# The router of a mixture-of-experts block rewritten: experts chosen by token blocks, one-pass count and slot products, overflow tables computed behind the first expert

## Chip, cores and metric

One core of one Trainium2 chip runs the whole kernel. The metric is device time in microseconds, median over runs. Lower is better.

## What is computed

`reference` runs two blocks. The first (a mixer with two kinds of linear attention and a SwiGLU layer) is not touched by the change. The second is a loop over two layers; each ends with a mixture of experts, and that is where the change lies. Cut to what matters:

```
x = _layernorm(alpha * x + mix, ln1_g, ln1_b)           # mix = merged @ w_o
grp_prob = softmax(xt @ w_rg + b_rg)                    # 4 groups
grp_p, grp_idx = top_k(grp_prob, 1)
exp_logits = (xt @ w_re + b_re).reshape(n_tok, 4, 8)    # 32 experts
in_grp = take_along_axis(exp_logits, grp_idx)           # the 8 of the chosen group
top_p, top_i = top_k(softmax(in_grp), 2)
weights = grp_p * top_p / sum(top_p)
expert_id = grp_idx * 8 + top_i                         # 2 experts for each of 512 tokens
# tokens are sorted by expert; each expert e: (silu(xe @ w_gate[e]) * (xe @ w_up[e])) @ w_down[e]
y = sum over the 2 of weights * row;  x = _layernorm(alpha * x + y, ln2_g, ln2_b)
```

## The kernel before

All engines run programs written out by hand in one order, tied by semaphores (`S(name)`). `LT` = 4 blocks of 128 tokens. A `rendezvous` makes each of PE, ACT, DVE and POOL drain, count up and wait until all four have come. `dr()` is a drain of DVE: it stands between operations that depend on each other.

**Output product (`wo_tile_pe`, `wo_tile_dve`).** The right half of `merged @ w_o` is made block by block: 24 matmuls of L193 for one block (products of high and low parts), then DVE adds the residual (L2488) and takes the statistics, ACT the root (L2548), and `ln_tile` on DVE normalizes (L2524 to L2529).

**Route (`route_pe`, `route_act`, `route_dve`, `route_pool`).** PE turns the normalized block over (`turn_tile`, L2569), ACT copies it to `hT` (L2552), and PE makes the logits with the 36 router columns as stationary side, so that they stand one logit to a partition; ACT adds the bias (L2543), and PE turns them back to one token to a partition (`back`, L2580). Only when all four blocks are back does DVE start (L2622): largest group (L2627 to L2630), the eight logits of that group (L2639 to L2644), their two largest (L2648 to L2651), the gates with two exponentials on ACT in between, and 0/1 rows over 32 experts (`oh`, `ohs`, up to L2667). PE counts the tokens that stand ahead of each in its expert (L2600, into `rank` and `cnt`). DVE works out from them the slot in the expert (`r_`), and for experts with more than `CAP` = 80 tokens an overflow block out of `OVER` = 12 (`over_*`, `o_`, `q_`), makes 0/1 matrices of slot and block (L2707 to L2711), and one product on PE (L168, 80x44) gives the table of tokens for each block. DVE makes two tables of it: `tok_tab` (which token's row is gathered) and `row_tab` (where the result is put). POOL clears `xg` and takes part in the rendezvous.

**Experts (`experts_*`).** After the rendezvous POOL gathers the token rows of the experts with indirect DMAs (L3165). SP brings the weights (3 MB for an expert) through a ring of four slots of 2 MB: the gate and up weights of an expert are requested when PE has finished with gate and up of the expert two before it (`up_passed`). ACT makes the high part of the weights (L2968, in two halves), DVE the low part (L3074), PE turns the gathered rows over (L2853), ACT and DVE split them (L2965, L3071), and PE does gate and up (`up`, 24 matmuls of L193). In `first()` DVE also makes the eight diagonal gate matrices (L3112), before it splits the weights of expert 1.

## Time and profile before

| what | us |
|---|---|
| median of 3 runs | 2833.71 |
| lowest and highest | 2823.22, 2834.99 |
| the profiled execution's own time | 2826.56 |
| its span in the profile | 2824.7 |
| route of layer 1, from the end of the last output block (DVE L2488) to the first expert's first matmul | 1466.05 to 1508.42 |
| the same in layer 2 | 2410.65 to 2451.13 |

The profile counts time from the start of the span. Layer 1 of the second block ends its route near 1508 and layer 2 near 2451; the same code stands in both, written out once for each. The share of PE that is busy (90% of the span) says little about the route, where PE has few and small matmuls.

### The profile page before, as it was taken

To read this page: it belongs to the slowest core of one execution; us is meant where nothing else is said; L and a number is where in the kernel's file an instruction comes from. 1 tells how busy PE (TensorE), PEld (TensorE's weight loads), DVE (VectorE), ACT (ScalarE), POOL (GpSimd) and SP (SyncE) were. 2 spreads that over 40 slices of the span, in tenths; PEclk is the share of its full clock that TensorE was granted. 3 is DMA by queue.
4 is the path that set the end of the run, shared out by engine and by line. 5 is a ranking of instruction groups with operands and counts; after the bars stand their busy time and mean duration, and the time that the engine had idled before them with its cause. 6 is when DMAs were issued, how large, how long until landed. Compare 5 with 4: busy or idle time off the path is not lost.

```text
span 2824.7 us, 31219 instructions
## 1 busy us (share of the span) xinstructions
PE 2535.3 (90%) x11284; PEld 1842.9 (65%) x11284; DVE 1582.7 (56%) x2277; ACT 1275.1 (45%) x1881; POOL 233.2 (8%) x201
## 2 busy tenths in 40 slices
PE   6899887799999899999986999978989999699996
PEld 2587664488878567588864666635857887466664
DVE  6546576322223467534456788745854445577775
ACT  5433544422222444533325777715354323377773
POOL 0000000000000010000002233201000000132320
PEclk9899998999999999999997999989999999799998
DMA  9412000222212302112134999851202213299994
GB/s 344 167 60 90 5 1 1 89 90 90 73 61 100 114 31 90 51 70 90 60 136 158 322 335 330 294 186 60 90 30 90 90 60 99 93 330 335 343 329 169
DMA packets 197748, 392.23 MB, mean 139 GB/s; under 512 B 23663, under 2 KB 54399, under 8 KB 197631
## 3 DMA queue, kind: packets, MB, share of 16 engines
q1 hardware_dynamic: 170912, 340.55, 34.3%
q10 hardware_dynamic: 14367, 33.34, 3.1%
q0 software_dynamic: 12352, 16.81, 1.9%
q8 instruction: 70, 1.15, 0.2%
q14 instruction: 47, 0.39, 0.0%
HBM read 386.44 MB, written 29.36 MB: 147 GB/s over the span
## 4 chain that ended last, share of the span: by engine, by line
PE 68%; DMA 10%; DVE 9%; ACT 5%; issue 4%; DVEq 2%; SPq 1%; ACTq 1%; POOL 0%; POOLq 0%; PEldq 0%; PEld 0%
PE banks L193 52%; PE banks L168 9%; DMA ring<-in_w_exp_up 8%; ACT hT_parts L2968 2%; DMA ring<-in_w_mod 1%; PE banks L1901 1%; PE banks L1909 1%; DVE hT_parts L3071 1%; DVE ring_parts L471 1%; PE banks L1926 1%; SPq L241 1%; DVE ring_parts L3074 1%; PE banks L2210 1%; PE banks L2197 1%; DVE x_res L2529 1%
## 5 line engine op out<-in xcount | busy, mean ns | idle before, releaser
L193 PE MATMUL banks<-hT_parts 128*128 128x512 f32 (+1 forms) x1376 | 548.7, 399 | 0.0
L193 PE MATMUL banks<-arena_parts,hT_parts 128*128 128x512 f32 (+1 forms) x1408 | 525.2, 395 | 17.4 <-DVEq L161 9.1
L193 PE MATMUL banks<-ring_parts,arena_parts 128*80 128x512 f32 (+2 forms) x1296 | 514.5, 397 | 0.0
L193 PE MATMUL banks<-hT_parts,arena_parts 128*128 128x512 f32 (+1 forms) x1248 | 447.3, 398 | 33.9 <-DVE hT_parts L3071 19.4
L193 PE MATMUL banks<-arena_parts,ring_parts 128*128 128x512 f32 (+1 forms) x1168 | 457.5, 392 | 0.0
L193 PE MATMUL banks<-arena_parts 128*128 128x512 f32 (+3 forms) x1280 | 408.9, 391 | 10.2 <-DVEq L161 8.7
L223 DVE TENSOR_TENSOR ring_parts<-ring,hT_parts 128x1024 fp32r<-128x1024 f32 x148 | 181.3, 1225 | 337.7 <-ACT hT_parts L219 333.8
L3074 DVE TENSOR_TENSOR ring_parts<-ring,hT_parts 128x2048 fp32r<-128x2048 f32 x128 | 292.9, 2289 | 125.4 <-ACT hT_parts L2968 125.3
L219 ACT ACTIVATE hT_parts<-ring 128x1024 fp32r<-128x1024 f32 x148 | 156.7, 1059 | 420.7 <-PE banks L193 419.9
L193 PEld LDWEIGHTS banks<-arena_parts,hT_parts 128*128 128x128 f32 x1408 | 267.2, 190 | 83.1 <-DVEq L161 18.4
L2968 ACT ACTIVATE hT_parts<-ring 128x2048 fp32r<-128x2048 f32 x128 | 244.4, 1911 | 166.2 <-DMA ring<-in_w_exp_up 114.3
L193 PEld LDWEIGHTS banks<-hT_parts 128*128 128x128 f32 (+1 forms) x1376 | 240.7, 175 | 83.1 <-issue 2.5
L193 PEld LDWEIGHTS banks<-hT_parts,arena_parts 128*128 128x128 f32 (+1 forms) x1248 | 216.3, 173 | 112.2 <-issue 33.7
L193 PEld LDWEIGHTS banks<-arena_parts 128*128 128x128 f32 (+2 forms) x1280 | 224.2, 175 | 81.5 <-DVEq L161 9.0
L193 PEld LDWEIGHTS banks<-ring_parts,arena_parts 128*80 128x80 f32 (+1 forms) x1296 | 215.7, 166 | 76.4 <-issue 2.3
L193 PEld LDWEIGHTS banks<-arena_parts,ring_parts 128*128 128x128 f32 x1168 | 220.5, 189 | 49.1
L3080 DVE TENSOR_TENSOR ring_parts<-ring,arena_parts 128x2048 fp32r<-128x2048 f32 x62 | 141.7, 2286 | 22.4 <-ACT arena_parts L2977 22.4
L168 PE MATMUL banks<-arena 128*128 128x128 f32 (+5 forms) x456 | 97.7, 359 | 49.0 <-DMA arena<-y_rows 18.8
L3165 POOL DMA_INDIRECT arena<-x_rows,arena x64 | 97.7, 1526 | 316.2 <-PE banks L2853 289.8
L2977 ACT ACTIVATE arena_parts<-ring 128x2048 fp32r<-128x2048 f32 x62 | 118.7, 1915 | 0.0
L168 PEld LDWEIGHTS banks<-arena 128*128 128x128 f32 (+3 forms) x456 | 66.8, 202 | 79.4 <-issue 40.9
L168 PE MATMUL banks<-ring,hT 128*128 128x512 f32 (+1 forms) x256 | 110.3, 591 | 8.6 <-POOLq L3232 4.3
(484 smaller groups left out, 3069.1 us busy)
## 6 DMA issues: line engine op xcount, KB each, us to landing
ring<-in_w_exp_gate SPq DMA_DIRECT2D x64, 1024.0 KB, 5.4
ring<-in_w_exp_up SPq DMA_DIRECT2D x64, 1024.0 KB, 8.2
ring<-in_w_exp_down SPq DMA_DIRECT2D x128, 512.0 KB, 6.8
ring<-in_w_in SPq DMA_DIRECT2D x58, 1024.0 KB, 7.3
ring<-in_w_mod SPq DMA_DIRECT2D x24, 1024.0 KB, 13.9
ring<-in_w_gate SPq DMA_DIRECT2D x11, 1024.0 KB, 5.4
ring<-in_w_up SPq DMA_DIRECT2D x11, 1024.0 KB, 8.1
ring<-in_w_down SPq DMA_DIRECT2D x22, 512.0 KB, 4.0
```

Of the source, the lines that this page charges most:

```text
L168: last = nc.tensor.matmul(out, l, r, start=(i == 0), stop=(i == len(pairs) - 1))
L193: last = nc.tensor.matmul(out, l, r, start=start and i == 0, stop=stop and i == len(products) - 1)
L219: nc.scalar.activation(hi_unit(s[1]), unit_of(ring, n, q), ACT.Copy).then_inc(S("unit_hi"), 1)
L223: nc.vector.tensor_tensor(unit_of(ring_r, n, q), unit_of(ring, n, q), hi_unit(s[1]).bitcast(F32), ALU.subtract).then_inc(S("unit_lo"), 1)
L241: sp.dma_start(dst, src).then_inc(S(f"chunk_in{n % SLOTS}"), 16)
L471: V.tensor_tensor(mod_half(ring_r, u, h), mod_half(ring, u, h), mod_hi[h].bitcast(F32), ALU.subtract).then_inc(S("mod_lo"), 1)
L1901: nc.tensor.matmul(out, q(h, i), k(h, w), start=True, stop=False)
L2968: return A_(ew_half(h), half_of(ring, n, h), ACT.Copy)
L2977: return A_(hi, dn_rows(ring, n), ACT.Copy)
L3074: return V.tensor_tensor(half_of(ring_r, n, h), half_of(ring, n, h), ew_half(h).bitcast(F32), ALU.subtract)
L3080: return V.tensor_tensor(dn_rows(ring_r, n), dn_rows(ring, n), hi.bitcast(F32), ALU.subtract)
L3165: return g.indirect_dma_start(out=xg[:, c, :], out_offset=None, in_=x_rows, in_offset=bass.IndirectOffsetOnAxis(ap=picked(tok_tab, tok_cur ...
```

## The change

It does these things:

- The router weights lie as 40 columns (4 groups, 4 unused, 32 experts), and are now the moving side: `logits` gives one token to a partition at once. The bias is a row that DVE adds. The two turns (`back`) and ACT's bias step go.
- `logits(i - 2)` stands in the middle of the output product of block i (`between`).
- `ln_tile` writes a block in two halves, and PE and ACT turn and copy by halves.
- `chosen_dve(a, b)` chooses for blocks a to b-1: block 0 ahead of the statistics of the last block, blocks 1 and 2 behind the last normalization, block 3 last. Outside the chosen group it adds -1e30, so that one search over 32 gives the expert itself.
- Counts and slots are one-pass products (`A_r` is float32r). `r_` (rank) leads directly to the slots, with no overflow in it; the product has 64 columns, tokens and rows apart.
- The two gathers of experts 0 and 1 are issued in `route_pool` ahead of the rendezvous, when `tok_tab` is there.
- The gates (`gates_dve`) and all that has to do with overflow (`over_dve`, `over_pe`, `over_tables_dve`) move into `first()` of the experts.

```diff
         def logits(i):
             ...
-                pe.wait_ge(S("m_copied"), i + 1)
-                mm(ps[0:36, 6 + i % 2, 0:P], [(w_rt[:, k, :], hT[:, k, tok_of(i)]) for k in range(KD)]).then_inc(S("lg_tok"), 1)
+                if i >= 2:
+                    pe.wait_ge(S("lg_read"), i - 1)
+                for k in range(KD):
+                    if k % 4 == 0:
+                        pe.wait_ge(S("m_copied"), 2 * i + k // 4 + 1)
+                    last = nc.tensor.matmul(ps[:, 6 + i % 2, 0:40], hT[:, k, tok_of(i)], w_rt[:, k, :], start=(k == 0), stop=(k == KD - 1))
+                last.then_inc(S("lg_acc"), 1)
...
             for i in range(LT):
-                wo_tile_pe(pe, i)
+                wo_tile_pe(pe, i, (lambda: logits(i - 2)) if i >= 2 else None)
                 if i:
                     turn_tile(i - 1)
-                if i >= 2:
-                    logits(i - 2)
             logits(LT - 2)
-            back(0)
-            back(1)
             turn_tile(LT - 1)
-            back(2)
             logits(LT - 1)
-            back(LT - 1).then_inc(S("lg_acc"), 1)
...
+        def tables(dve, tok, row, c0, c1):
+            V = nc.vector
+            V.tensor_scalar(tok_f32[:, c0:c1], tok, -1.0, floor_c[0:CAP, :], ALU.add, ALU.max)
+            dve.drain()
+            V.tensor_copy(tok_tab[:, c0:c1], tok_f32[:, c0:c1])
+            dve.drain().then_inc(S("tabbed" if c0 == 0 else "ov_tabbed"), 1)
+            V.tensor_scalar(row_f32[:, c0:c1], row, -1.0, None, ALU.add)
             ...
         def route_dve(dve):
             ...
             for i in range(1, LT):
-                ln_tile(dve, "ln1", i - 1)
+                ln_tile(dve, "ln1", i - 1, 2)
+                if i == LT - 1:
+                    dve.wait_ge(S("wrt_in"), 4 * 16)
+                    chosen_dve(dve, 0, 1)
                 wo_tile_dve(dve, i)
+            ln_tile(dve, "ln1", LT - 1, 2)
+            chosen_dve(dve, 1, LT - 1)
+            dve.wait_ge(S("slots_in"), 1)
+            chosen_dve(dve, LT - 1, LT)
             ...
             dve.wait_ge(S("rank_acc"), 1)
+            V.tensor_tensor(rt_t.rearrange("p (t j) e -> p t j e", j=2), oh,
+                            ps[:, 5, 0:NE * LT].rearrange("p (t n) -> p t n", t=LT)[:, :, None, :].to_broadcast([P, LT, 2, NE]), ALU.mult)
             dr()
             V.tensor_reduce(r_, rt_t, AX.X, ALU.add)
             dr()
+            V.tensor_tensor(pl_oh, slot_rank[:, None, :].to_broadcast([P, 2 * LT, CAP]), r_[:, :, None].to_broadcast([P, 2 * LT, CAP]), ALU.is_equal)
+            dr().then_inc(S("placed"), 1)
+            V.tensor_copy(cnt, ps[:, 5, NE * LT:NE * (LT + 1)])
+            dve.wait_ge(S("tab_acc"), 1)
+            tables(dve, ps[0:CAP, 4, 0:NE], ps[0:CAP, 4, NE:2 * NE], 0, NE)
...
+        def over_pe(pe):
+            pe.wait_ge(S("ov_placed"), 1)
+            for j in range(2 * LT):
+                last = nc.tensor.matmul(ps[0:CAP, 7, 0:2 * OVER], pl_oh[:, j, :], bl_over[:, j, :, :].rearrange("p a n -> p (a n)"),
+                                        start=(j == 0), stop=(j == 2 * LT - 1))
+            last.then_inc(S("ov_tab"), 1)
...
         def route_pool(pool):
-            pool.wait_ge(S("chosen"), 1)
+            pool.wait_ge(S("wo_free"), LT)
             nc.gpsimd.iota(slot_rank, ...).then_inc(S("slots_in"), 1)
             nc.gpsimd.memset(xg, 0.0)
             pool.drain()
             pool.wait_ge(S("rows_out"), LT * 16)
+            pool.wait_ge(S("tabbed"), 1)
+            gather_rows(pool, tok_tab[:, 0:1].bitcast(U32), 0).then_inc(S("xg_in0"), 16)
+            gather_rows(pool, tok_tab[:, 1:2].bitcast(U32), 1).then_inc(S("xg_in1"), 16)
...
             def first():                                # experts_pe
                 ...
                 turn_h(0, 0)
+                over_pe(pe)
...
             def first():                                # experts_dve
                 for h in range(2):
                     w_lo(0, 0, h)
                 x_lo(0, 0)
+                gates_dve(dve)
                 for j in range(2):
                     for i in range(LT):
                         V.tensor_scalar(e_diag[:, j * LT + i, :], ident[:, :], e_w[:, j, i:i + 1], None, ALU.mult)
                 dve.drain().then_inc(S("diag_full"), 1)
+                over_dve(dve)
                 w_lo(1, 1, 0)
                 mult(0, 0)
                 x_lo(1, 1)
                 w_lo(1, 1, 1)
                 h_lo(0, 0)
+                over_tables_dve(dve)
```

On PE, in the program of before, block 1 of the normalized tokens is turned over behind the output product of block 2, and the logits of block 0 follow (L168 with `hT` and the router weights in the arena):

```order
L193 MATMUL banks<-arena_parts 128x512
L2569 MATMUL banks<-ident,x_res 128x128
L2569 MATMUL banks<-ident,x_res 128x128 x7
L168 MATMUL banks<-hT,arena 36x128
L168 MATMUL banks<-hT,arena 36x128 x7
L193 MATMUL banks<-arena_parts 128x512
```

In the changed program the logits of block 0 stand between the matmuls of block 2, and the turn is in halves (L2578 are the logits, L2566 the turn):

```order
L193 MATMUL banks<-arena_parts 128x512
L2578 MATMUL banks<-arena,hT 128x40
L2578 MATMUL banks<-arena,hT 128x40 x3
L2578 MATMUL banks<-arena,hT 128x40
L2578 MATMUL banks<-arena,hT 128x40 x3
L193 MATMUL banks<-arena_parts 128x512
```

The logits of each block moved to half an output block earlier; those of block 1 now stand ahead of the end of block 3's product, where one set of logits stood ahead of it before.

On DVE, in the program of before, the first expert begins with the two halves of its weights and its rows (L3074, L3071), then come the eight gate diagonals and the weights of expert 1:

```order
L3074 TENSOR_TENSOR ring_parts<-ring,hT_parts 128x2x1024
L3071 TENSOR_TENSOR hT_parts<-banks,arena_parts 128x640
L3112 TENSOR_SCALAR arena<-ident,arena 128x128 x8
L3074 TENSOR_TENSOR ring_parts<-ring,hT_parts 128x2x1024
L3077 TENSOR_TENSOR arena<-hT,banks 80x256
```

In the changed program (L3155 are the diagonals, L3113 the rows) the gates stand ahead of them and the overflow work (24 operations, L2724 to L2758) behind them:

```order
L3113 TENSOR_TENSOR hT_parts<-banks,arena_parts 128x640
L2711 TENSOR_REDUCE arena<-arena 128x4
L2712 TENSOR_SCALAR arena<-arena 128x4
L2714 TENSOR_TENSOR arena<-arena 128x4
L2716 RECIPROCAL arena<-arena 128x4
L2718 TENSOR_TENSOR arena<-arena 128x4
L3155 TENSOR_SCALAR arena<-ident,arena 128x128 x8
L2724 TENSOR_TENSOR arena<-arena,past 128x192
L2725 TENSOR_TENSOR arena<-arena,past 128x48
L2727 TENSOR_REDUCE arena<-arena 128x32
```

All of this moved from ahead of the rendezvous to ahead of the split of expert 1's weights.

On POOL, in the program of before, the gathers follow the rendezvous; in the changed program the first two stand ahead of it, and nothing else lies between:

```order
L2775 IOTA arena 128x80
L2776 MEMSET arena 80x2048
L2784 DMA arena<-x_rows,arena 80x1024
L2784 DMA arena<-x_rows,arena 80x1024
L2784 DMA arena<-x_rows,arena 80x1024
```

The first two DMA rows are the ones that moved past the rendezvous.

## Rows read from the trace of the kernel before

**Rows 1.** Page, the chain that ended last, shares by engine.

```profile
PE 68%; DMA 10%; DVE 9%; ACT 5%; issue 4%; DVEq 2%; SPq 1%; ACTq 1%; POOL 0%; POOLq 0%; PEldq 0%; PEld 0%
```

**Rows 2.** Chain in order of time, one turn among the experts: start, length, what.

```profile
1722.40 8.20 DMA ring<-in_w_exp_up
...
1736.13 5.81 PE banks L193 x24
1742.59 8.11 DMA ring<-in_w_exp_up
```

**Rows 3.** Stretches of layer 1: length, busy us of each engine, clock, DMA share.

```profile
1486.30:1489.10 2.80, 2.77 (x12) 2.63 (x12) 0.00 (x0) 0.00 (x0) 2.11 (x2) 0.50 0.00 0
1489.10:1496.50 7.40, 0.01 (x1) 0.01 (x1) 6.24 (x22) 0.00 (x0) 0.00 (x0) 0.50 0.00 0
...
1560.00:1800.00 240.00, 227.06 (x1076) 150.73 (x1075) 190.12 (x144) 179.63 (x165) 77.21 (x48) 0.99 0.93 331
```

**Rows 4.** DVE in order of time, layer 1: start, length, operation, idle before.

```profile
1466.05 0.69 DVE L2488 SCALAR_TENSOR_TENSOR x_res<-x_res,banks 128x512 f32<-128x512 f32 x1 [2.50 <-PE banks L193]
...
1469.82 0.16 DVE L2524 RECIPROCAL stat<-stat 128x1 f32<-128x1 f32 x1 [2.02 <-ACT stat L2548]
...
1471.24 1.28 DVE L2529 SCALAR_TENSOR_TENSOR x_res<-x_res,stat,arena 128x1024 f32<-128x1024 f32 x1
1479.24 0.17 DVE L2622 COPY arena<-banks 128x16 f32<-128x16 f32 x1 [6.72 <-PE banks L2580]
...
1485.96 0.28 DVE L2667 TENSOR_TENSOR arena<-arena 128x128 f32<-128x128 f32 x1
1489.13 0.29 DVE L2670 COPY arena<-banks 128x128 f32<-128x128 f32 x1 [2.89 <-PE banks L2600]
...
1491.47 0.42 DVE L2686 TENSOR_REDUCE arena<-arena 128x8 f32<-128x256 f32 x1
...
1494.06 0.17 DVE L2703 TENSOR_TENSOR arena<-arena 128x8 f32<-128x8 f32 x1
1494.30 0.17 DVE L2705 TENSOR_TENSOR arena<-arena 128x8 f32<-128x8 f32 x1
...
1494.98 0.82 DVE L2709 TENSOR_TENSOR arena<-arena 128x640 f32<-128x640 f32 x1
...
1498.89 0.20 DVE L2727 TENSOR_SCALAR arena<-banks 80x44 f32<-80x44 f32 x1 [0.27 <-PE banks L168]
...
1515.65 2.29 DVE L3074 TENSOR_TENSOR ring_parts<-ring,hT_parts 128x2048 fp32r<-128x2048 f32 x1 [5.72 <-ACT hT_parts L2968]
```

**Rows 5.** PE, ACT, POOL and SP in order of time, layer 1.

```profile
1496.49 2.37 PE L168 MATMUL banks<-arena 128*80 128x44 f32 x16 [7.39 <-DVEq L2712]
...
1508.42 0.71 PE L193 MATMUL banks<-hT_parts,arena_parts 128*80 128x512 f32 x1 [1.65 <-DVE hT_parts L3071]
...
1500.57 3.71 ACT L2968 ACTIVATE hT_parts<-ring 128x2048 fp32r<-128x2048 f32 x2 [16.12 <-DVEq L161]
...
1501.35 1.07 POOL L3165 DMA_INDIRECT arena<-x_rows,arena  x1 [12.90 <-DVEq L161]
1502.73 2.99 POOL L3165 DMA_INDIRECT arena<-x_rows,arena  x1 [0.30 <-issue]
...
1526.68 0.39 SPq L241 DMA_DIRECT2D ring<-in_w_exp_gate  x1
```

**Rows 6.** Layer 2, DVE, ACT and POOL in order of time.

```profile
2410.65 0.69 DVE L2488 SCALAR_TENSOR_TENSOR x_res<-x_res,banks 128x512 f32<-128x512 f32 x1 [2.46 <-PE banks L193]
...
2451.00 1.64 DVE L3112 TENSOR_SCALAR arena<-ident,arena 128x128 f32<-128x128 f32 x8
...
2443.79 3.71 ACT L2968 ACTIVATE hT_parts<-ring 128x2048 fp32r<-128x2048 f32 x2 [16.13 <-DVEq L161]
...
2445.82 0.96 POOL L3165 DMA_INDIRECT arena<-x_rows,arena  x1 [0.30 <-issue]
```

**Rows 7.** Groups of PE by form: busy us, mean ns of one.

```profile
L168 PE MATMUL banks<-hT 128*128 128x64 f32 x128 | 16.0, 278 | 0.6
```

348 lines of the change are left out of this document (175 added, 173 removed).

## The prediction

> **What bounds the kernel now.** I read the chain that ended last first. By engine PE holds 68% of it [rows 1], which points away from the route: there the chain must be followed in order of time. Among the experts it goes round between PE's gate and up (5.81 us), a weight transfer (8.20 and 8.11 us) and ACT's high part, and one turn, two experts, takes 1742.59 - 1722.40 = 20.2 us [rows 2]. The stretches say why: from 1560 to 1800 the DMA engines are 93% busy at 331 GB/s [rows 3]. So this stage runs at the rate of its weights, and it ends when its stream has started, plus the bytes. That stream starts when gate and up of expert 1 are done: SP requests the weights of expert 3 at 1526.68 [rows 5]. In the route the DMA is idle (share 0.00, 1486 to 1496) and PE nearly so [rows 3]: one engine waits for the next. What the route loses or gains up to the end of expert 1's gate and up therefore reaches the end of the kernel, in each of two layers. That is where the sum has to be made.
>
> Timeline of the route in layer 1 [rows 4, 5], from the end of the last output block (1466.05, called T): root there at T + 3.8 (1469.82), block normalized 2.70 later (1472.5), logits back at 1479.24, choice done at 1486.24 (end of L2667), counts back 1489.13, slots given to PE 1496.49, table back 1498.89, first expert's first matmul 1508.42. T to that matmul (called M): 42.4 us. In layer 2, T is 2410.65 and M 2451.1 (start of L3112 plus 0.1): 40.5 us [rows 6].
>
> **Part by part, in the time behind T.**
>
> *Logits inside the output product: +2.0.* Before, one set of logits stood ahead of the end of block 3's product; now there are two. A set is 16 passes with a 128x128 stationary side and few columns; the nearest row has 128 of them at 64 columns, 16.0 us busy, 0.125 us each [rows 7], so 2.0 us. T moves back by that. The turn by halves lets PE start each block earlier by at most half of L2529 (0.6 us); I count nothing for it.
>
> *Root of block 3: 2.75 in place of 3.8.* DVE's statistics take 1.75. ACT was held until then by the copy and bias of block 2; now two half copies and one DMA issue, done about 2.4 behind T; then root and semaphore 0.32.
>
> *Normalization: 2.75* (2.70 and a second instruction start).
>
> *Choice: 6.35 behind the normalization, in place of 13.7 (1472.5 to 1486.24).* A small dependent step of DVE costs 0.24 us (L2703 to L2705, 1494.06 to 1494.30 [rows 4]), an independent one beside it 0.08. One block has 11 steps up to its `ohs`: 2.65 us. Blocks 1 and 2 together, some operations twice and the two products with the token numbers behind them: 3.7. Block 0 (2.9 us) lies in DVE's idle time ahead of the last output block (2.50 us before [rows 4], some 3.6 with the logits in it): hidden, and if that cover were missing it would cost at most 2.9. The turn, copy and logits of block 3 (about 3 us on PE and ACT) are hidden behind the 3.7 of blocks 1 and 2; even at the low clock they are.
>
> *Counts: 0.6 in place of 2.9.* Only the last two one-pass products wait for block 3. 12 passes took 2.77 [rows 3], 0.23 each at granted clock 0.50, the 1.2 GHz level.
>
> *Slots: 2.0 in place of 7.4.* Of the 22 operations between 1489.1 and 1496.5 three stay: product with the ranks (0.49 with its drain), sum (0.49, from L2686's 0.42), slot matrix (0.82 + 0.1) [rows 4].
>
> *Table product: 1.3 in place of 2.4*: 8 passes for 16, which took 2.37 [rows 5].
>
> *Table for the gather: 0.5*: two dependent steps on 80x32.
>
> *Rendezvous: +3.4. Here a wait comes in.* DVE needs 1.0 more for the row table, but POOL now issues two gathers before it arrives. Its first gather started at 1501.35, about 0.9 behind the end of DVE's tables; then 1.07, 0.30, 0.96 for the second (layer 2's row), and 0.15 to leave: 3.4 [rows 5, 6]. Queued behind POOL's arrival are all engines; ACT's split of expert 0's weights is first. The gathers come early, but nobody can use them.
>
> *Split of the first expert: 7.5.* ACT begins, two low parts on DVE, split of the rows: 2443.79 to 2451.00, plus 0.1 to M and 0.15 to start [rows 6]. Before, the tables and the rendezvous took 1.7 from the product to ACT's start; then 7.85 (1500.57 to 1508.42 [rows 5]) in layer 1, where the late rows cost 0.5.
>
> Sum behind T: 2.0 + 2.75 + 2.75 + 6.35 + 0.6 + 2.0 + 1.3 + 0.5 + 3.4 + 7.5 = 29.15. M comes 42.4 - 29.15 = 13.2 earlier in layer 1 and 40.5 - 29.15 = 11.3 in layer 2.
>
> *Overflow and gates behind M: 2.6 given back in each layer.* From 1509.9 on, DVE was idle for 5.72 us before it split expert 1's weights [rows 4]. Into that gap go the gates (five operations, four drains: 1.1) and the overflow work: 24 operations in 11 dependent steps, among them one of 640 elements (0.82) and three of 256 to 384; by the same rows 6.3. 7.4 - 5.7 = 1.7 us late for `w_lo(1, 1, 0)`; behind it wait `mult(0, 0)`, `turn_h` and expert 1's rows, and so PE's `up(1)`. On PE `over_pe` (8 passes, 1.2 us) now stands directly ahead of `up(1)`, which is ready 0.3 later than `turn_h`: 0.9 more. `over_tables_dve` (1.6 us) sits behind `h_lo(0, 0)`; the next on DVE is the down weights' low part, which PE wants only after `up(1)` and a turn (8 us): hidden.
>
> Net: 13.2 + 11.3 - 2 x 2.6 = **19.3 us**. The profiled execution took 2826.56 us (span 2824.7), so its counterpart is 2807.3. It lay 7 us under the median; the mean of the four executions shown is 2829.6, and I forecast 2829.6 - 19.3 = **2810**.
>
> *Bounds of what the trace does not show.* POOL's drain behind a gather: between nothing beyond 0.15 and the whole landing of the second, about 3 us more; I take 0.15, since POOL went on to the next gather in 0.30. If POOL could arrive when the second gather has only been handed over, 0.96 less. The small operations have rows, but new shapes: 0.20 to 0.30 for a step over about 45 dependent ones on the path, -1.8 to +2.7 a layer. Logits 0.117 (the old ones) to 0.22 a pass: -0.1 to +1.5. Together a gain of 12 to 24.
>
> **A rule weighed against a row.** The gather of 2.99 us in layer 1 began at 1502.73, just behind the start of DVE's L3074, and ended when the first of these two operations was over and a free gather's time had passed; its twin in layer 2 took 0.96 [rows 5, 6]. The Trainium skill (SBUF — State Buffer, "Who interferes with whom") says that copy, cast and tensor_scalar on DVE may hold GpSimd out of the shared port pair, and that tensor_tensor should not disturb the writing of descriptors; the row speaks against its second half. By its first half the row table, whose operations now run beside the first gather, could hold POOL up: all five together under 0.9 us, a gain of 17.5 instead of 19.3. By the row, the split does not run beside the two first gathers any more, and each takes about 1 us, as summed.
>
> **Rivals.**
>
> *A, the gain is mostly given back (0.24).* PE's clock: the first twelve passes of expert 0 ran at the low level. If `up(1)`, after a longer idle time of PE behind over_dve, runs wholly at 1.2 GHz, its 24 matmuls take 24 x 0.43 = 10.2 instead of 7.4: 2.8 a layer. With DVE's steps at 0.30 (2.7) the gain is 19.3 - 11 = 8: 2821. For it: the granted clock is 0.50 through the whole route [rows 3]. Against: there is less idle time ahead of M than before, and the level rose in time in both layers.
>
> *B, more than summed (0.12).* POOL arrives at once when the gathers are handed over (saves 2), and the overflow work fits the gap (saves 1.7 a layer): 19.3 + 5.4 = 25, 2805. For it: layer 2 shows the split path without waits. Against: POOL's gather is shown as busy time.
>
> *C, nothing moves (0.04).* If the stage's end were set by bytes requested before the route ended, an earlier start would be absorbed: 2830. Against: requests wait for PE's gate and up, and the DMA is idle in the route [rows 3].
>
> *D, slower (0.06).* The write of the last block's rows to `x_rows` now starts behind two ACT copies, about T + 8.6, and shares the DMA with expert 2's weights. POOL waits for it before the gathers, and since these now stand ahead of the rendezvous, all engines wait. It costs from the point where it lands behind T + 18.25, that is takes over 9.6 us, and turns the change slower than before where it takes over 19 us: with 25 us it costs 15.4 a layer against 9.6 gained, 2841. Against: nothing else large is in the queue then.
>
> My own case has the remaining 0.54.
>
> **How the numbers follow.** 0.5% of this kernel is 14 us, about what a measurement can tell from no change. My case spans a gain of 12 to 24 and lies over 14 in nine of ten: 0.49; with B, 0.61; faster 0.62. Same: the tenth of my case, most of A, and C: 0.32. Slower: D, 0.06. Executions of one kernel differ by 12 us, so the range reaches from B (2805) less 8 to A (2821) plus 6: 2797 to 2827; D and the end of C stand outside, less than 2 in 10.
>
> **What the profile of the changed kernel would show.** `up(1)` ends, and SP requests expert 3's weights, about 10 us earlier relative to T in each layer; three DVE operations between counts and slots; ACT's first L2968-like operation 3.3 to 3.5 us behind the cast of `tok_tab`, with POOL as last to arrive, and gathers landed before PE turns them; DVE without a gap between the diagonals and expert 1's weights; `over_pe` just ahead of `up(1)`. An end of `up(1)` that moves less than 7 us, or a stage whose length changes by more than 2 us behind it, would make the prediction wrong.

## The result, and the profile of the changed kernel

The changed kernel took 2816.69 us in the median of 5 runs (2813.12 to 2822.70), the kernel before 2831.82 us in 5 runs (2823.22 to 2834.99): ratio 0.995, 95% interval 0.9931 to 0.9969, some 15 us. The profiled executions stand 12.95 us apart (2826.56 and 2813.61; spans 2824.7 and 2811.9).

I read the trace by marks instead of by its span, because the parts outside the route, which no edit touches, move by 1 to 5 us from one execution to another. U is the start of ACT's last gate activation ahead of the output product. T, the end of the last output block, and M, the first expert's first gate and up matmul, are as in the prediction. S is SP's request of expert 3's weights. "Cast" is the end of the cast that completes `tok_tab`, "ACT" the start of its first split. S - U is what the change did to a layer. All in us, layer 1 / layer 2:

| kernel | T - U | cast - T | ACT - cast | M - T | S - M | S - U | span |
|---|---|---|---|---|---|---|---|
| before | 52.75 / 51.83 | 34.27 / 32.89 | 0.25 / 0.25 | 42.37 / 40.48 | 18.26 / 18.01 | 113.38 / 110.32 | 2824.7 |
| changed | 54.74 / 54.34 | 16.30 / 17.21 | 6.88 / 5.01 | 30.48 / 29.52 | 21.07 / 20.59 | 106.29 / 104.45 | 2811.9 |

S came 7.1 and 5.9 us earlier behind U: 13.0 together, as much as the spans differ. From S of layer 1 to U of layer 2 it took 832.1 and 831.0 us, from S of layer 2 to the end 355.6 and 356.1. So the request did set the end of the stage, and what was gained up to it arrived.

The new chain, DVE of the changed kernel in order of time (start, length, operation, idle before and its releaser), answers to [rows 4]. T is the first row:

```profile
1468.73 0.69 DVE L2491 SCALAR_TENSOR_TENSOR x_res<-x_res,banks 128x512 f32<-128x512 f32 x1 [0.20 <-PE banks L193]
...
1473.70 0.30 DVE L2625 TENSOR_TENSOR arena<-banks,arena 128x40 f32<-128x40 f32 x2
...
1477.72 0.19 DVE L2625 TENSOR_TENSOR arena<-banks,arena 128x40 f32<-128x40 f32 x1
...
1481.32 0.42 DVE L2696 TENSOR_TENSOR arena<-arena,banks 128x256 f32<-128x256 f32 x1 [0.27 <-PE banks L2590]
...
1482.31 0.82 DVE L2701 TENSOR_TENSOR arena_parts<-arena 128x640 fp32r<-128x640 f32 x1
...
1484.85 0.18 DVE L2661 CAST arena<-arena 80x32 int32<-80x32 f32 x1
...
1493.93 4.49 DVE L3116 TENSOR_TENSOR ring_parts<-ring,hT_parts 128x2048 fp32r<-128x2048 f32 x2 [7.69 <-ACT hT_parts L3010]
```

The choice of blocks 1 and 2 starts at 1473.70, that of block 3 at 1477.72 with no wait; three operations (1481.32 to 1483.13) stand where 22 stood. Up to the cast (1485.03) the whole is as long as summed (its parts are compared further down). Then comes an idle time of 7.69 us ahead of L3116 that the sum did not have in this size. The other engines, answering to [rows 5], show who is late:

```profile
1499.21 0.71 PE L193 MATMUL banks<-hT_parts,arena_parts 128*80 128x512 f32 x1 [6.03 <-DVE hT_parts L3113]
...
1491.91 3.71 ACT L3010 ACTIVATE hT_parts<-ring 128x2048 fp32r<-128x2048 f32 x2 [10.49 <-POOLq L161]
...
1486.03 1.07 POOL L2784 DMA_INDIRECT arena<-x_rows,arena  x1 [14.43 <-DVEq L2662]
1487.41 0.97 POOL L2784 DMA_INDIRECT arena<-x_rows,arena  x1 [0.31 <-issue]
1494.04 3.00 POOL L2784 DMA_INDIRECT arena<-x_rows,arena  x1 [5.66 <-PE banks L2894]
...
1520.28 0.39 SPq L241 DMA_DIRECT2D ring<-in_w_exp_gate  x1
```

POOL's second gather is over at 1488.38, and ACT, which waits for POOL at the rendezvous, starts at 1491.91, 3.5 us later. In layer 2 the gather ends at 2426.08 and ACT starts at 2427.88, 1.8 us later:

```profile
2425.12 0.96 POOL L2784 DMA_INDIRECT arena<-x_rows,arena  x1 [0.30 <-issue]
...
2427.88 3.71 ACT L3010 ACTIVATE hT_parts<-ring 128x2048 fp32r<-128x2048 f32 x2 [8.62 <-POOLq L161]
```

The same two gathers in the view of the DMA issues (the last number is us from issue to landing; each window holds only the second gather, first of layer 1, then of layer 2):

```profile
arena<-x_rows,arena POOLq DMA_INDIRECT x1, 4.3
arena<-x_rows,arena POOLq DMA_INDIRECT x1, 2.5
```

1487.41 + 4.3 = 1491.7 and 2425.12 + 2.5 = 2427.6: ACT starts 0.2 and 0.3 us behind the landings. That is the upper bound of the prediction ("the whole landing of the second"), not the 0.15 it took.

A second thing is visible ahead of T, on ACT. The kernel before, DMA issues for router and normalization rows behind the gate activation at U, then ACT's next operation, and the table load for the root:

```profile
1413.30 0.69 ACT L2429 ACTIVATE arena<-banks,cols 128x512 f32<-128x512 f32 x1 [2.07 <-PE banks L193]
...
1414.41 0.54 ACTq L2535 DMA_DIRECT2D arena<-in_b_router_group  x1
1414.97 0.65 ACTq L2536 DMA_DIRECT2D arena<-in_b_router_expert  x1
...
1417.56 2.20 ACT L228 ACTIVATE arena_parts<-arena 128x512 fp32r<-128x512 f32 x4 [3.58 <-issue]
...
1446.41 1.28 ACT L2548 ACT_TABLE_LOAD   x1 [13.62 <-DVE arena L2518]
```

and the changed kernel, where L2540 and L2541 bring the bias as a row for all 128 partitions:

```profile
1413.99 0.69 ACT L2432 ACTIVATE arena<-banks,cols 128x512 f32<-128x512 f32 x1 [2.10 <-PE banks L193]
...
1415.10 1.86 ACTq L2540 DMA_DIRECT2D arena<-in_b_router_group  x1
1416.99 0.80 ACTq L2541 DMA_DIRECT2D arena<-in_b_router_expert  x1
...
1419.54 2.19 ACT L228 ACTIVATE arena_parts<-arena 128x512 fp32r<-128x512 f32 x4 [4.87 <-issue]
...
1434.81 1.28 ACT L2547 ACT_TABLE_LOAD   x1
```

The six issues hold ACT's next operation until 5.54 us behind U instead of 4.26 (layer 2: 5.20 for 3.20). The first output block ends 32.67 and 32.32 us behind U instead of 31.28 and 30.44. And the table load, on the path behind block 0's statistics before, lies 12 us ahead of them now.

### The profile page after: what moved, and what is told of

It is laid out like the page before. It is cut to its first block, busy times and chain, and to the rows that moved or that the text cites. A ratio compares the mean times of both kernels' runs of the same rounds, so it can differ in the third digit from the quotient of the medians.

```text
span 2811.9 us, 31299 instructions
## 1 busy us (share of the span) xinstructions
PE 2534.3 (90%) x11266; PEld 1842.8 (66%) x11266; DVE 1594.4 (57%) x2329; ACT 1272.4 (45%) x1881; POOL 241.0 (9%) x201
## 4 chain that ended last, share of the span: by engine, by line
PE 68%; DMA 10%; DVE 9%; ACT 5%; issue 4%; DVEq 2%; ACTq 1%; SPq 1%; POOLq 0%; POOL 0%; PEldq 0%; PEld 0%
PE banks L193 52%; PE banks L168 8%; DMA ring<-in_w_exp_up 8%; ACT hT_parts L3010 2%; DMA ring<-in_w_mod 1%; PE banks L1902 1%; PE banks L1910 1%; DVE ring_parts L3116 1%; DVE hT_parts L3113 1%; DVE ring_parts L471 1%; PE banks L1927 1%; PE banks L2211 1%; SPq L241 1%; PE banks L2198 1%; DVE arena L3119 0%
## 5 line engine op out<-in xcount | busy, mean ns | idle before, releaser
L193 PE MATMUL banks<-arena_parts,hT_parts 128*128 128x512 f32 (+1 forms) x1408 | 525.6, 395 | 18.4 <-DVEq L161 8.7
L223 DVE TENSOR_TENSOR ring_parts<-ring,hT_parts 128x1024 fp32r<-128x1024 f32 x148 | 183.4, 1239 | 335.1 <-ACT hT_parts L219 331.2
L3116 DVE TENSOR_TENSOR ring_parts<-ring,hT_parts 128x2048 fp32r<-128x2048 f32 x128 | 292.8, 2288 | 120.6 <-ACT hT_parts L3010 120.2
L2784 POOL DMA_INDIRECT arena<-x_rows,arena x64 | 105.8, 1653 | 336.1 <-PE banks L2894 305.7
L168 PE MATMUL banks<-arena 128*128 128x128 f32 (+4 forms) x424 | 94.2, 363 | 34.1 <-DMA arena<-y_rows 18.5
L168 PE MATMUL banks<-ring,hT 128*128 128x512 f32 (+1 forms) x256 | 110.1, 589 | 8.6 <-POOLq L3272 4.4
L3213 POOL DMA_INDIRECT y_rows<-arena x64 | 93.4, 1460 | 192.2 <-ACT arena L3022 179.0
```

The source lines that it names most:

```text
L168: last = nc.tensor.matmul(out, l, r, start=(i == 0), stop=(i == len(pairs) - 1))
L193: last = nc.tensor.matmul(out, l, r, start=start and i == 0, stop=stop and i == len(products) - 1)
L223: nc.vector.tensor_tensor(unit_of(ring_r, n, q), unit_of(ring, n, q), hi_unit(s[1]).bitcast(F32), ALU.subtract).then_inc(S("unit_lo"), 1)
L2784: return nc.gpsimd.indirect_dma_start(out=xg[:, c, :], out_offset=None, in_=x_rows, in_offset=bass.IndirectOffsetOnAxis(ap=at, axis=0), bo ...
L3116: return V.tensor_tensor(half_of(ring_r, n, h), half_of(ring, n, h), ew_half(h).bitcast(F32), ALU.subtract)
L3213: return g.indirect_dma_start(out=y_rows, out_offset=bass.IndirectOffsetOnAxis(ap=picked(row_tab, row_cur, b, c), axis=0), in_=yb[:, c, :] ...
```

## The experiments

Each is the changed kernel with one edit, except the last. Marks, layer 1 / layer 2:

| kernel | T - U | cast - T | ACT - cast | M - T | S - M | S - U | span |
|---|---|---|---|---|---|---|---|
| e1_join_first | 56.28 / 54.39 | 16.82 / 17.22 | 1.36 / 1.30 | 25.48 / 25.82 | 21.47 / 20.81 | 103.23 / 101.02 | 2805.0 |
| e2_gathers_behind | 54.65 / 54.24 | 16.94 / 17.53 | 1.28 / 1.29 | 26.12 / 26.17 | 21.03 / 20.08 | 101.80 / 100.49 | 2808.5 |
| e3_bias_late | 53.97 / 52.45 | 16.55 / 17.02 | 6.86 / 5.07 | 30.71 / 29.39 | 20.77 / 21.14 | 105.45 / 102.98 | 2812.4 |
| e4_no_overflow | 54.90 / 56.20 | 16.93 / 16.66 | 6.68 / 5.00 | 30.91 / 28.96 | 18.38 / 18.15 | 104.19 / 103.31 | 2816.1 |
| e5_over_in_gap | 54.05 / 54.27 | 17.39 / 17.55 | 6.88 / 5.06 | 31.57 / 29.91 | 17.51 / 17.30 | 103.13 / 101.48 | 2809.2 |
| e6_choose_three | 54.06 / 54.26 | 18.79 / 19.73 | 6.66 / 5.01 | 32.75 / 32.39 | 21.29 / 20.62 | 108.10 / 107.27 | 2820.2 |
| e7_logits_behind | 52.70 / 52.51 | 16.29 / 16.60 | 6.65 / 5.03 | 30.24 / 28.93 | 21.16 / 21.44 | 104.10 / 102.88 | 2812.6 |
| e8_wait_back | 54.63 / 54.94 | 16.93 / 17.49 | 6.88 / 5.03 | 31.11 / 29.82 | 21.85 / 20.02 | 107.59 / 104.78 | 2821.9 |
| e10_one_gather | 54.05 / 54.41 | 17.04 / 16.97 | 5.25 / 3.60 | 29.59 / 27.87 | 20.36 / 20.00 | 104.00 / 102.28 | 2811.1 |
| e11_best | 52.22 / 50.66 | 16.29 / 17.90 | 1.36 / 1.31 | 24.95 / 26.51 | 18.24 / 17.26 | 95.41 / 94.43 | 2799.8 |

A mark that an edit does not touch moves between kernels: T - U by about 1 us as a rule, cast - T from 16.3 to 17.4 and from 16.6 to 17.9 (twice outliers in T - U: 56.28 in e1, 56.20 in e4). Only differences beyond that are read, and where they stand in one layer alone the text says so.

Some expectations named spans too. These are single executions, and executions of the kernel before differ by 12 us, so a span does not test an edit worth 2 to 5 us. By the number alone e1 came near what was expected (2805.0 for 2803), e2 between its expectation and its rival (2808.5; 2804 to 2805 against 2812), and e3 and e4 missed it (2812.4 for 2808 to 2809; 2816.1 for 2806.6).

**e1_join_first.** POOL drains and counts itself up ahead of the gathers, and waits for the others behind them:

```diff
-            pool.drain()
+            passed["pool"] = passed.get("pool", 0) + 1
+            pool.drain().then_inc(S("stage_done"), 1)
             pool.wait_ge(S("rows_out"), LT * 16)
             pool.wait_ge(S("tabbed"), 1)
             gather_rows(pool, tok_tab[:, 0:1].bitcast(U32), 0)...
             gather_rows(pool, tok_tab[:, 1:2].bitcast(U32), 1)...
+            pool.wait_ge(S("stage_done"), 4 * passed["pool"])
...
-                    rendezvous(pool, "pool")
```

> Edit: POOL counts itself into the rendezvous before it waits for the table, and issues the two gathers after that; the others no longer wait for its drain. Theory 1 (POOL's drain behind the gathers waits for the rows to land, and holds all engines): ACT's first weight split starts 1.2 to 1.5 us behind the end of the token table's cast (6.9 and 5.0 in the changed kernel); the first expert's first matmul comes 5.6 us earlier in layer 1 and 3.7 in layer 2, and the span falls by about 9 us, from 2811.9 to 2803. Rival (the wait is not POOL's: the late start is ACT's or DVE's own, or the weight stream absorbs it): the span stays above 2808.

Measured: ACT starts 1.36 and 1.30 us behind the cast, and M comes 5.0 and 3.7 us earlier behind T (5.5 and 3.7 behind the cast). ACT, DVE and POOL of e1, layer 1:

```profile
1487.78 3.71 ACT L3012 ACTIVATE hT_parts<-ring 128x2048 fp32r<-128x2048 f32 x2 [4.97 <-DVEq L161]
...
1494.20 0.82 DVE L3115 TENSOR_TENSOR hT_parts<-banks,arena_parts 128x640 fp32r<-128x640 f32 x1
...
1487.42 1.07 POOL L2786 DMA_INDIRECT arena<-x_rows,arena  x1 [14.95 <-DVEq L2662]
```

ACT is released by DVE (the last table) now, and splits while the gathers run. The second row shows which of the two chains is the later one: DVE splits the rows (L3115) with no idle time, right behind the low parts of the weights. So the rows are there in time, and the split of the weights sets M, 7.30 us behind ACT's start in both layers, as in the changed kernel.

**e2_gathers_behind.** The two gathers go back behind the rendezvous:

```diff
-            pool.wait_ge(S("tabbed"), 1)
-            gather_rows(pool, tok_tab[:, 0:1].bitcast(U32), 0).then_inc(S("xg_in0"), 16)
-            gather_rows(pool, tok_tab[:, 1:2].bitcast(U32), 1).then_inc(S("xg_in1"), 16)
...
+            rows(0, 0).then_inc(S("xg_in0"), 16)
+            rows(1, 1).then_inc(S("xg_in1"), 16)
             gather(2, 0)
```

> Edit: the two gathers behind the rendezvous again, as in the kernel before; all else as in the changed kernel. Theory 1: ACT starts 1.2 to 1.5 us behind the cast; the rows of expert 0 are now the last to come (gather 2.0 us behind the cast, 2.5 to 4.1 to land, turn, two splits), so the first matmul stands 9.0 to 9.9 us behind the cast in place of 14.2 and 12.3: 4.3 and 3.3 us earlier, the span 2804 to 2805. Rival (issuing the gathers early is worth something even with the wait): the span is 2812 or more.

Measured: M - T 26.12 and 26.17, that is 4.4 and 3.4 us less than with the gathers ahead. Behind the cast, from where the edit acts, M stands at 9.18 and 8.64 (14.18 and 12.31 in the changed kernel, 8.66 and 8.60 in e1); layer 2 is below the 9.0 to 9.9 expected. DVE of e2, layer 1:

```profile
1495.39 0.82 DVE L3110 TENSOR_TENSOR hT_parts<-banks,arena_parts 128x640 fp32r<-128x640 f32 x1 [0.52 <-ACT arena_parts L3004]
```

Here, and not in e1, the split of the rows is waited for. This one part of the change cost more than it could bring: issued ahead without the drain behind them (e1) the gathers are worth 0.5 us in layer 1 and nothing that can be told in layer 2 (0.04).

**e10_one_gather.** Only expert 0's gather ahead of the rendezvous, expert 1's first behind it:

```diff
             gather_rows(pool, tok_tab[:, 0:1].bitcast(U32), 0).then_inc(S("xg_in0"), 16)
-            gather_rows(pool, tok_tab[:, 1:2].bitcast(U32), 1).then_inc(S("xg_in1"), 16)
...
+            rows(1, 1).then_inc(S("xg_in1"), 16)
             gather(2, 0)
```

> Only the gather of expert 0's rows stands ahead of the rendezvous; expert 1's is issued behind it. If POOL's drain waits until the data of the gathers ahead of it have landed, ACT's first split starts about as late behind the cast of the token table as one gather takes with its landing: POOL's 1.0 us, and 2.5 to 4 us from there, that is 3.5 to 5.1 us (now 6.88 and 5.01, with two gathers; 1.3 when the drain stands ahead of both). Rival: the drain waits only until POOL has handed the gather over; then ACT starts 2.0 to 2.2 us behind the cast, and the 6.88 and 5.01 come from the second gather or from something else.

Measured: 5.25 and 3.60 us, the first just over the range. POOL and ACT of e10, layer 1, and in the view of the DMA issues the landing of that gather:

```profile
1488.09 1.08 POOL L2783 DMA_INDIRECT arena<-x_rows,arena  x1 [15.17 <-DVEq L2662]
...
1492.34 3.71 ACT L3009 ACTIVATE hT_parts<-ring 128x2048 fp32r<-128x2048 f32 x2 [8.86 <-POOLq L161]
```

```profile
arena<-x_rows,arena POOLq DMA_INDIRECT x1, 4.0
```

1488.09 + 4.0 = 1492.1, and ACT starts at 1492.34; in layer 2 the issue is at 2425.32, landing 2.4 later, ACT at 2427.98, again 0.2 behind. The end of the gather's own row on POOL (1489.17 and 2426.33) lies 3.2 and 1.7 us ahead of ACT's start, so it is no mark of it. The same holds for e3, e4, e5, e6 and e8, which have both gathers ahead of the drain: seven kernels, fourteen places, always 0.2 to 0.3 behind the landing of the last gather ahead of the drain. So the drain waits for the data; the rival had 2.0 to 2.2 from the cast.

**e3_bias_late.** The two bias DMAs move from the middle of the gate stage behind ACT's last copy of the output weights (`bias_load` holds the two lines taken out of `route_load`):

```diff
             for q in range(4):
                 nc.scalar.activation(wo_hi[:, q, :, :], wo_unit(ring, q), ACT.Copy)...
+            bias_load(act, lay)
```

> Edit: ACT issues the two transfers of the bias row behind its split of the output weights, not ahead of the split of the merged activations. Theory 2 (the row form of the bias, spread over 128 partitions, costs ACT issue time on the path): the time from the first router transfer's issue to ACT's next operation falls from 5.5 and 5.2 us to about 3, PE resumes 1.3 and 1.9 us earlier, span 2808 to 2809. Rival (the issues are slow because the queue is full, whatever stands in it): the two transfers of the normalization rows take the time instead, and the span stays at 2811 or more.

Measured: ACT's next operation stands 3.91 and 3.05 us behind U (5.54 and 5.20 with the bias). In layer 2 T - U falls by 1.9, clear of the scatter, and the first output block ends 30.45 us behind U, as in the kernel before (30.44): the issues were on the path there. In layer 1 T - U falls by 0.8 to 53.97, which e5, e6 and e10 have with the bias in its old place (54.05), so no gain is shown. The four DMAs that spread a row over 128 partitions took 0.5 to 1.9 us each of ACT's queue in the changed kernel (4.3 and 4.0 us together), the bias as a column 0.54 and 0.65. But it is not the shape alone: at their new place the same two bias DMAs took 0.34 and 0.45, and in layer 1 the two rows of the normalization rose from 1.14 and 0.50 to 1.87 and 0.86. The rival has a part in layer 1; what makes an issue slow in the middle of the gate stage was not found.

**e4_no_overflow.** Left out: the overflow work. `over_dve`, `over_pe` and `over_tables_dve` go; two tables are set to zero in their place, so no expert has an overflow block.

```diff
-                over_pe(pe)
...
-                over_dve(dve)
+                V.memset(ove_f, 0.0)
+                V.memset(go_f, 0.0)
+                dve.drain()
+                V.tensor_copy(ove_i, ove_f)
+                V.tensor_copy(go_i, go_f)
+                dve.drain().then_inc(S("over_ready"), 1)
...
-                over_tables_dve(dve)
```

> Edit: leaves out the overflow work (ranks over 80, blocks 32 to 43 of the tables): the number of overflow blocks is set to 0, the small PE product and the second tables go. Theory 3 (the overflow work does not fit DVE's gap, and its product stands ahead of expert 1's gate and up): from the first expert's first matmul to the request of expert 3's weights it takes 18.2 us in each layer in place of 21.1 and 20.6, span 2811.9 - 5.3 = 2806.6. Rival (PE's clock makes the difference): the stretch stays over 20 us, or its change shows in the 24 matmuls of expert 1.

Measured: S - M 18.38 and 18.15 against 21.07 and 20.59, and 18.26 and 18.01 before. The overflow work behind the first expert costs 2.7 and 2.4 us, the 2.6 of the sum. The span does not show it: it is 4.2 us longer than the changed kernel's, of which 2.4 lie ahead of U of layer 1 and 3.8 behind S of layer 2 (359.9 for 356.1), where the edit changes nothing that these rows show. DVE waits again ahead of expert 1's weights:

```profile
1509.60 2.29 DVE L3115 TENSOR_TENSOR ring_parts<-ring,hT_parts 128x2048 fp32r<-128x2048 f32 x1 [4.23 <-ACT hT_parts L3009]
```

**e5_over_in_gap.** Gates and diagonals to the end of the experts, the overflow work alone in the gap, `over_pe` ahead of the turn of h:

```diff
                 x_lo(0, 0)
-                gates_dve(dve)
-                for j in range(2):
-                    for i in range(LT):
-                        V.tensor_scalar(e_diag[:, j * LT + i, :], ...)
-                dve.drain().then_inc(S("diag_full"), 1)
                 over_dve(dve)
...
                 h_lo(b, 1)
+                gates_dve(dve)
+                for j in range(2):
+                    for i in range(LT):
+                        V.tensor_scalar(e_diag[:, j * LT + i, :], ...)
+                dve.drain().then_inc(S("diag_full"), 1)
...
-                turn_h(0, 0)
                 over_pe(pe)
+                turn_h(0, 0)
```

> The gates and the eight diagonals leave first() and stand behind h_lo(b, 1) at the end of the experts on DVE; over_dve now fills the whole gap of DVE behind x_lo(0, 0), and over_pe stands ahead of turn_h(0, 0). If the 2.6 us given back behind M come from DVE being late for w_lo(1, 1, 0) and from over_pe standing directly ahead of up(1), then from M to SP's request of expert 3's weights it takes 18.2 us again (now 21.1 and 20.6), and the request comes 2.4 to 2.9 us earlier in each layer, some 5 us in the span. Rival 1: the overflow work is still late, and it stays over 20 us. Rival 2: gates and diagonals cost their 3 us at the end of the experts; then the request moves but the span does not.

Measured: 17.51 and 17.30, 3.5 and 3.3 less, more than expected. DVE and PE of e5:

```profile
1507.21 2.29 DVE L3116 TENSOR_TENSOR ring_parts<-ring,hT_parts 128x2048 fp32r<-128x2048 f32 x1 [0.40 <-ACT hT_parts L3010]
...
1508.66 0.72 PE L2764 MATMUL banks<-arena_parts 128*80 128x24 f32 x8
1509.89 0.36 PE L2904 MATMUL banks<-ident,arena 80*128 80x80 f32 x2 [0.51 <-DVE arena L3119]
```

ACT is the later one again ahead of L3116 (0.40 idle), 6.5 us behind M, where it was 9.4 in the changed kernel (7.2 before), and `over_pe` (L2764) fills PE's wait for the turn instead of standing behind it. Whether gates and diagonals cost anything at the end stays open: in layer 1 the stretch from S to the first weights of the next stage (`w_in`) is 329.5 us (329.8 changed, 330.3 before), but the span fell by 2.7, not by the 6.1 of S - U. Of the rest 2.1 us lie between S of layer 2 and the end (358.2 for 356.1); e4 and e8, which leave gates and diagonals where they were, have 359.9 and 359.0 there, so the scatter of this stretch is enough to explain it.

**e6_choose_three.** Blocks 1 to 3 in one call of `chosen_dve`, once the logits of block 3 are there:

```diff
-            pe.wait_ge(S("chosen"), 3)
+            pe.wait_ge(S("chosen"), 2)
...
-            chosen_dve(dve, 1, LT - 1)
             dve.wait_ge(S("slots_in"), 1)
-            chosen_dve(dve, LT - 1, LT)
+            chosen_dve(dve, 1, LT)
```

> Blocks 1, 2 and 3 are chosen in one go, when the logits of block 3 are there; block 0 stays where it is. If the choice by blocks gains because blocks 1 and 2 (3.7 us by the sum) run while PE and ACT make the last logits, the cast of the token table ends about 1.0 to 1.5 us later behind T in each layer (about 3 us of waiting for the last logits, then one set of some 3.8 us in place of 3.7 and 2.65), and counts get longer by 0.2. Rival: one set for two saves as much as the waiting costs, and the cast stays within 0.4 us of where it was (16.3 and 17.2 behind T).

Measured: the cast ends 2.5 us later behind T in both layers, clear of the rival and 1 us more than I expected. DVE of e6:

```profile
1475.85 0.30 DVE L2625 TENSOR_TENSOR arena<-banks,arena 128x40 f32<-128x40 f32 x2
1479.88 0.20 DVE L2625 TENSOR_TENSOR arena<-banks,arena 128x40 f32<-128x40 f32 x1 [3.73 <-PE banks L2578]
...
1484.33 0.35 DVE L2654 TENSOR_TENSOR arena_parts<-arena,tok_f 128x192 fp32r<-128x192 f32 x1
...
1485.97 0.42 DVE L2695 TENSOR_TENSOR arena<-arena,banks 128x256 f32<-128x256 f32 x1 [1.14 <-PE banks L2590]
```

From the first operation of the choice (L2625) to the product with the ranks (1485.97) it takes 10.12 us, where the changed kernel takes 1481.32 - 1473.70 = 7.62. The wait for the last logits is 3.73 us, and the counts are late too: 1.14 us of idle ahead of the last row, 0.27 in the changed kernel, because more of their products wait for the one choice. In return three blocks in one set take 4.7 us, where the two sets take 7.1. So the choice by blocks is worth 2.5 us a layer (in layer 2 the same stretch takes 11.07 for 8.56).

**e7_logits_behind.** `logits(i - 2)` behind the turn, as in the kernel before:

```diff
-                wo_tile_pe(pe, i, (lambda: logits(i - 2)) if i >= 2 else None)
+                wo_tile_pe(pe, i)
                 if i:
                     turn_tile(i - 1)
+                if i >= 2:
+                    logits(i - 2)
```

> The logits of block i - 2 go back behind the turn of block i - 1, as in the kernel before; so only one set stands ahead of the end of block 3's product, where now there are two. If a set costs 1.87 us of PE on the path and the last sets have cover in DVE's choice, T comes 1.5 to 2.0 us earlier behind the start of the output product, and the cast stays where it is behind T. Rival: the set that has moved is now on the path behind T (blocks 1 and 2 wait for it, or the last turn does), and the cast ends as much later behind T as T came earlier.

Measured: T - U falls by 2.0 and 1.8 (from the end of the first output block to T by 1.8 in both layers), and the cast comes no later behind T (16.29 and 16.60). DVE of the changed kernel and of e7 between the third output block and T:

```profile
1460.48 0.69 DVE L2491 SCALAR_TENSOR_TENSOR x_res<-x_res,banks 128x512 f32<-128x512 f32 x1 [3.29 <-PE banks L193]
...
1468.73 0.69 DVE L2491 SCALAR_TENSOR_TENSOR x_res<-x_res,banks 128x512 f32<-128x512 f32 x1 [0.20 <-PE banks L193]
```

```profile
1454.96 0.69 DVE L2491 SCALAR_TENSOR_TENSOR x_res<-x_res,banks 128x512 f32<-128x512 f32 x1 [0.62 <-PE banks L193]
1461.43 0.69 DVE L2491 SCALAR_TENSOR_TENSOR x_res<-x_res,banks 128x512 f32<-128x512 f32 x1 [1.52 <-PE banks L193]
...
1469.66 0.69 DVE L2491 SCALAR_TENSOR_TENSOR x_res<-x_res,banks 128x512 f32<-128x512 f32 x1 [0.17 <-PE banks L193]
```

Both kernels take 8.2 us for the last block, with a set of logits in it. The block ahead of it takes 6.47 in e7 and 8.24 in the changed kernel (1452.24 to 1460.48). A set costs 1.87 us on PE, and setting it earlier buys nothing. The set that has moved, that of block 1, stands behind T now, in one row with that of block 2 on PE:

```profile
1470.78 3.66 PE L2578 MATMUL banks<-arena,hT 128*128 128x40 f32 x32
...
1475.69 1.95 PE L2578 MATMUL banks<-arena,hT 128*128 128x40 f32 x16 [0.28 <-ACT hT L2550]
```

Both are done at 1474.44, just ahead of DVE's choice of blocks 1 and 2, which starts 4.95 us behind T (4.97 in the changed kernel): root and normalization of block 3 cover them. Nor does block 3's set come later, 7.98 us behind T for 8.78: it took 1.95 us, where the changed kernel's took 2.88, with the granted clock at 1.00 from 1475 to 1478 for 0.57 there.

**e8_wait_back.** The wait for the router weights stands at the head of `route_act` again:

```diff
         def route_act(act, lay):
             A_ = nc.scalar.activation
+            act.wait_ge(S("wrt_in"), 4 * 16)
```

> ACT waits for the router weights at the head of the route again, as in the kernel before (which waited for them there to add the bias). If the 1.28 us table load for the root now lies hidden only because no wait stands ahead of it, this wait puts it back on the path of the first block: T comes 1.2 to 1.3 us later behind the start of the output product in each layer, and nothing else moves. Rival: the table load is moved by the compiler for another reason or its cost was never on the path; then T stays where it is within 0.3 us.

Measured: the wait does move the table load back. ACT of e8, then DVE:

```profile
1449.33 1.28 ACT L2548 ACT_TABLE_LOAD   x1 [13.70 <-DVE arena L2521]
...
1447.50 0.69 DVE L2491 SCALAR_TENSOR_TENSOR x_res<-x_res,banks 128x512 f32<-128x512 f32 x1 [3.66 <-PE banks L193]
...
1470.16 0.69 DVE L2491 SCALAR_TENSOR_TENSOR x_res<-x_res,banks 128x512 f32<-128x512 f32 x1 [0.19 <-PE banks L193]
```

But T does not move by 1.3. From the first output block to T it takes 22.66 and 22.62 us, against 22.07 and 22.02 in the changed kernel: 0.6. PE has the products of blocks 0 and 1 back to back and turns block 0 only then, which covers half of the load. The expectation is missed by half, and T - U shows none of it in layer 1, because the six issues happened to take 0.76 less there.

**e11_best.** All that helped in one kernel: e1, e5 and e7, and all six DMA issues behind the copies of the output weights:

```diff
-                if j == 7:
-                    route_load(act, lay)
-                    ln_load(act, lay, "ln1")
...
             for q in range(4):
                 nc.scalar.activation(wo_hi[:, q, :, :], wo_unit(ring, q), ACT.Copy)...
+            route_load(act, lay)
+            ln_load(act, lay, "ln1")
```

> All that helped, in one kernel: POOL drains and counts itself up for the rendezvous ahead of its gathers; gates and diagonals at the end of the experts, over_dve alone in the gap of DVE, over_pe ahead of turn_h(0, 0); logits(i - 2) behind the turn; all six DMA issues for router and normalization rows behind ACT's wo_hi copies instead of in the middle of the gate stage. Singly they moved the request of expert 3's weights by 5.0 and 3.7 (join), 3.5 (gap), 2.0 and 1.85 (logits), and the issues by 5.5 and 5.2 at most, of which only what lay ahead of PE's next product counts (1 to 4). If they add up, the request comes some 11 to 14 us earlier in each layer than in the changed kernel and the median is 2787 to 2795. Rival: they share one cover (DVE's choice, or the weights of expert 1), and together they bring less than 8 a layer: a median over 2800.

Measured: S - U 95.41 and 94.43, 10.9 and 10.0 us less than in the changed kernel, just under the 11 to 14 expected. The edits add up (singly 10.5 and 8.8 without the issues), but moving all six issues brings no more than moving the two of the bias: ACT's next operation stands 0.58 us behind U instead of 5.3, yet the first output block ends 32.01 and 30.45 us behind U, as in e3 (31.96 and 30.45). Something else holds it then, which was not looked for. T - U is 0.5 and 1.9 less than in e7. The median of 6 runs is 2798.96 us (2788.88 to 2806.19) against 2833.05 for the kernel before in 10 runs: ratio 0.9876, interval 0.9857 to 0.9895. That is a gain of 34 us, where the change brings 15. The median missed the 2787 to 2795: of 20.9 us by the marks 12.1 show in the spans. From S of layer 1 to U of layer 2 this execution took 835.8 us (the others 831 to 835), and from S of layer 2 to the end 358.8 (355.6 to 359.9). Whether this is the scatter of these stretches (e8, with the gates in their old place, has 835.1 and 359.0) or a price of the moved gates is not settled.

## Why the prediction was right, and which terms were not

The forecast was 2810 with a range of 2797 to 2827; 2816.69 lies in it. The gain was put at 19.3 us and came out at 13.0 by the marks, 12.95 by the profiled executions and 15.1 by the medians, inside the 12 to 24 of my own case. That is two thirds of the gain that was summed; the forecast started from 2829.6 for the kernel before, which then had a median of 2831.82.

- **What bounds the kernel** held. S came 13 us earlier, and both stretches behind it kept their length within 1.1 us. Rival C (nothing moves) is out. But my own sign of being wrong, an end of `up(1)` that moves by less than 7 us, is half met. Behind T it moved 9.1 and 8.4 us; behind U, which takes in what T itself lost and is how the sum adds up, 7.1 and 5.9. In layer 2 the gain fell short of what I had called the least.
- **Logits, +2.0 in T.** T - U moved by +1.99 and +2.51. That 1.99 meets 2.0 is luck, for most of it has another reason. From the first output block to T it is only +0.6 (22.07 for 21.47): the set costs 1.87 (2.0 in the sum), 0.6 comes back because the table load left the path (e8), and the rest, about 0.65, from the turn by halves and the bias step that left ACT, not separated further. The remaining 1.4 and 1.9 lie ahead of the first output block, with ACT's issues 1.3 and 2.0 longer, which the prediction did not have. In layer 2 e3 shows that they are the bias rows; in layer 1 it gives back no more than the scatter.
- **Root, normalization, choice, counts, slots, product, table: 16.25.** Measured cast - T 16.30 in layer 1, with errors that cancel: the root took 2.21 for 2.75, the choice 7.20 for 6.35 (4.02 and 3.18 for the 3.7 and 2.65 of its two sets), counts 0.42 for 0.6, slots 1.90 for 2.0; normalization, product and table are within 0.01. In layer 2 17.21: "even at the low clock they are" hidden was wrong there. The last turn and logits took 1.73 + 3.49 us on PE against 1.27 + 2.88, the granted clock being 0.67 from 2410 to 2412 and 0.50 from there (1.00 up to 1475 in layer 1). DVE waited 0.54 for them, plus 0.38 later:

```profile
2411.65 3.49 PE L2578 MATMUL banks<-arena,hT 128*128 128x40 f32 x16
...
2415.24 0.20 DVE L2625 TENSOR_TENSOR arena<-banks,arena 128x40 f32<-128x40 f32 x1 [0.54 <-PE banks L2578]
```

- **Rendezvous, +3.4: the term that was mis-sized.** I took 0.15 for POOL's drain behind the gathers, "since POOL went on to the next gather in 0.30". Going on to the next gather says nothing of a drain. It waits for the landing, 3.5 and 1.8 us beyond the end of the second gather (e1, e2, e10). The cost from the cast to ACT's start was 6.9 and 5.0. The bound that the prediction gave beside it, "about 3 us more", had it right for layer 1. The Trainium skill (Perfetto Trace Analysis, "DMA Instruction — SWDGE (GPSIMD)") says that the row of such a DMA ends when its descriptors are written, not when the data has moved; the traces agree: the row ends at 1488.38, the data is there at 1491.7. The row that I read could not show the landing, and the column of the issues that shows it was there.
- **Split 7.5**: 7.30 in both layers.
- **Overflow and gates, 2.6 given back**: 2.8 and 2.6 by S - M; e4 returns it to 18.4 and 18.15. DVE was 2.2 and 2.1 us late for `w_lo(1, 1, 0)` (1.7 in the sum), which leaves 0.65 and 0.47 for the rest (0.9 in the sum).
- **Rivals.** A (up(1) wholly at the low clock): its first 9 matmuls took 0.63 or so, then 0.40, and all 24 took 7.3 us, the 7.4 of my own case, so it does not hold, and DVE's steps stayed at 0.24. What spoke for A was misread: the clock is not 0.50 "through the whole route"; in the kernel before it was 0.83 from 1466 to 1486 and 0.50 only from there on. What was lost against the sum came from the drain, and in layer 2 from the choice and T too. B would have needed POOL to arrive when the gathers are handed over, and the overflow work to fit the gap, neither of which came; e1 makes the first and more. D: the last write of rows was issued at T + 5.8, ahead of the 8.6 assumed, landed 6.2 us later (3.9 in the kernel before), and so 4 us ahead of the cast; the gathers began 1.0 us behind the cast: nothing was held. My reason, "nothing else large is in the queue then", was wrong: the DMA share from 1472 to 1482 is 0.94 to 1.05, with gate and up weights that SP requests at T (1468.77 and 1469.19). Nor is the DMA idle in all of the route, only from 1486 to 1496, where it was read.

So each layer's error is 3.54 and 2.86 us: the drain 3.3 and 1.4 of it (less the 0.2 that the split was shorter), cover in the choice 0.05 and 0.96, T 0 and 0.5, overflow 0.2 and 0.

## What to carry to other kernels

A DMA that is moved ahead of a barrier is paid for in full if its issuer drains behind it: let that engine drain and count itself up first, issue, and wait for the others last. An early issue is worth only what the next engine was waiting for it (here 0.5 us in one layer, nothing in the other), so ask first who would use the data sooner. Deferred work goes where its engine waits, counted with what already stands in the gap: DVE's 9.4 us of gates, diagonals and overflow did not fit into the 7.2 between M and expert 1's weights, the overflow work alone did. And the issues of a DMA queue on a computing engine are part of that engine's program: read the time of each at the place where it stands, since the same bias row took 1.86 us at one place and 0.34 at another.
